# Two-layer PEER decoder step: turns of one gathered row instead of two, and weights formed at the end of a row's own turn

## What is computed

```python
# layer 0 mixer
z = gelu(x @ w_in); u, v = split(z); v = layer_norm(v)
y = (u * (tril(w_s) @ v + bias)) @ w_out
# layer 1 mixer
b, c, h = split(x @ w_in); z = c * h
y = (b * conv3(z)) @ w_out
# PEER, both layers, per token
q = (x @ w_query).reshape(8 heads, 2, 128)
s = q . sub_keys                       # 128 keys on each of 2 sides
sv, si = top_k(s, 16)                  # each side
cv, ci = top_k(all 16*16 sums, 16)     # 16 experts of 16384 per head
idx = i1 * 128 + i2;  g = softmax(cv)
a = gelu(expert_u[idx] . x)
out = sum over 8 heads, 16 experts of  g * a * expert_v[idx]
```

## Time and profile before

| what | value |
|---|---|
| runs | 1817.57, 1815.79, 1817.54 us; median 1817.54 |
| the profiled execution | 1816.76 us; span 1814.9 us |
| mean granted TensorE clock in it | 0.799 of full speed |
| TensorE, VectorE, ScalarE, GpSimd busy | 75%, 67%, 16%, 38% of the span |
| gathered by the indirect DMAs | 604.02 MB in 576 rows |
| moved in all | 718.27 MB |

### The profile page before, as it was taken

How to read it: one execution, slowest core, us unless ns; L and a number is a source line. 1 busy time by engine, 2 the same in 40 slices (tenths; PEclk the granted TensorE clock), 3 DMA queues, 4 the chain that set the end, 5 groups by cost and what they waited for, 6 DMA issues and landing times.

```text
span 1814.9 us, 23000 instructions
## 1 busy us (share of the span) xinstructions
PE 1358.0 (75%) x8388; PEld 644.8 (36%) x8388; DVE 1219.2 (67%) x3197; ACT 289.8 (16%) x970; POOL 684.7 (38%) x580
## 2 busy tenths in 40 slices
PE   8997989988946978776664498788765666776743
PEld 6884556644601744521110176356111111111100
DVE  1238867655648868678887656566888965555565
ACT  1111231102112202111111111021111100000011
POOL 0013423333223423344545533433444444444453
PEclk9998999999965989977665599989876667666655
DMA  9749999999999999999999999999999999999996
GB/s 381 293 154 422 381 362 393 356 422 420 409 423 417 380 421 421 420 410 422 408 422 393 421 340 418 422 418 420 407 421 411 397 421 421 421 421 421 417 420 282
DMA packets 100657, 718.27 MB, mean 396 GB/s; under 512 B 12064, under 2 KB 12576, under 8 KB 13600
## 3 DMA queue, kind: packets, MB, share of 16 engines
q0 software_dynamic: 82944, 604.02, 81.2%
q1 hardware_dynamic: 17184, 112.19, 15.2%
q10 hardware_dynamic: 416, 0.60, 0.1%
HBM read 715.24 MB, written 1.52 MB: 395 GB/s over the span
## 4 chain that ended last, share of the span: by engine, by line
DMA 48%; PE 34%; DVE 8%; issue 6%; DVEq 2%; POOL 2%; ACT 1%; another core or an unknown queue 0%; SPq 0%; POOLq 0%
DMA uvring<-expert_uv_dram,idx 43%; PE psum L649 11%; PE psum L660 11%; DMA wring<-w_chunks_dram 5%; PE psum L779 4%; PE psum L692 3%; DVE uvring L1190 2%; POOL uvring L601 2%; DVE diag L1203 1%; PE psum L731 1%; PE psum L762 1%; PE psum L759 1%; PE psum L668 1%; PE psum L641 1%; DVEq L993 1%
## 5 line engine op out<-in xcount | busy, mean ns | idle before, releaser
L601 POOL DMA_INDIRECT uvring<-expert_uv_dram,idx x576 | 684.5, 1188 | 1108.0 <-PE psum L649 872.9
L1190 DVE SCALAR_TENSOR_TENSOR uvring<-uvring,xn 128x1024 f32<-128x1024 f32 x576 | 705.5, 1225 | 413.0 <-DMA uvring<-expert_uv_dram,idx 394.1
L649 PE MATMUL psum<-uvring,diag 64*64 64x512 f32 x4096 | 709.6, 794 | 315.6 <-DVE diag L1203 305.7
L649 PEld LDWEIGHTS psum<-uvring,diag 64*64 64x64 f32 x4096 | 137.6, 159 | 805.2 <-DVE diag L1203 718.6
L908 ACT ACTIVATE a_gelu<-a_raw 128x1 f32<-128x1 f32 x576 | 114.8, 202 | 1205.7 <-DVE uvring L1190 1203.0
L660 PE MATMUL psum<-xT,wring 128*128 128x160 f32 (+1 forms) x1696 | 236.6, 298 | 27.5 <-DMA wring<-w_chunks_dram 26.5
L660 PEld LDWEIGHTS psum<-xT,wring 128*128 128x128 f32 x1696 | 223.2, 196 | 70.0 <-DMA wring<-w_chunks_dram 38.0
L1203 DVE TENSOR_SCALAR diag<-twin,a_gelu,gate 128x64 f32<-128x64 f32 x512 | 159.4, 311 | 26.8 <-ACT a_gelu L908 24.4
L641 PE MATMUL psum<-uvring,diag 128*32 128x256 f32 x512 | 68.9, 634 | 90.6 <-DVE diag L1203 85.7
L828 ACT ACTIVATE arena<-psum 128x160 f32<-128x160 f32 (+2 forms) x160 | 46.1, 298 | 225.6 <-PE psum L660 179.4
L779 PE MATMUL psum<-wring,arena 128*128 128x256 f32 x288 | 70.3, 400 | 3.4 <-DMA wring<-w_chunks_dram 2.3
(11 more groups left out here) (117 smaller groups left out, 836.1 us busy)
## 6 DMA issues: line engine op xcount, KB each, us to landing
wring<-w_chunks_dram SPq DMA_DIRECT2D x73, 1024.0 KB
uvring<-w_chunks_dram SPq DMA_DIRECT2D x15, 1024.0 KB, 9.8
kept<-w_chunks_dram SPq DMA_DIRECT2D x12, 1024.0 KB, 15.6
uvring<-expert_uv_dram,idx POOLq DMA_INDIRECT x576
x<-x_tok_dram SPq DMA_DIRECT2D x2, 512.0 KB, 4.6
uvring<-ln_gain_dram SPq DMA_DIRECT2D x1, 1024.0 KB, 28.5
uvring<-ln_bias_dram SPq DMA_DIRECT2D x1, 1024.0 KB, 28.9
keys<-sub_keys_dram SPq DMA_DIRECT2D x2, 512.0 KB, 9.7
```

The source lines that it names most:

```text
L601: pool.indirect_dma_start(uvring[:, n % RING, :], None, expert_uv, bass.IndirectOffsetOnAxis(ap=idx[t][:, i:i + 1], axis=0),).then_inc(uv_ ...
L649: mm = nc.tensor.matmul(acc[64 * j:64 * j + 64, 512 * i:512 * (i + 1)], diag[64 * i:64 * i + 64, place % DIAGS, :], row[64 * i:64 * i + 64 ...
L1190: nc.vector.scalar_tensor_tensor(out=uvring[:, slot, 0:D], in0=uvring[:, slot, 0:D], scalar=1.0, in1=xn[t][:, :], op0=ALU.mult, op1=ALU.mu ...
```

## The change

A turn becomes one row. `ROOM` is given per row, smaller than half of what a pair had, and a step that overdraws an engine's room is paid back from the next turns (`credit`); unused room isn't kept. VectorE takes at most one routing part in two turns, and one in each turn when the due turn is near. In turn p the engines now run:
- VectorE: dot p, steps, weights p.
- ScalarE: gelu p, steps.
- TensorE: row p (the first row of a tile waits for the next turn), steps.

So the weights of a row stand behind its own dot and behind the turn's steps, where they stood behind the next row's dot. A score read waits for part 1 of the routing that last read these scores (a new semaphore, `scanned`), and the planner knows of it. Code that could put a row's v half on VectorE (`VEC`, `add_v`, `wgt`), which no row used, is gone. The ring, the gathers, the chunks and the arithmetic are the same. The diff, cut to its core:

```diff
@@ -114,6 +104,15 @@
 
     heads = HEADS if t < 2 else FHEADS
     return ([(0, 1), (1, 1)] if (l, t) == (0, 0) else [(0, 2)]) + [(i, 2) for i in range(2, heads, 2)]
+
+
+def scanned_before(l, t, first, count):
+
+    before = [(l, 0) if t == 1 else (l - 1, 2 if t == 2 else 1)][0]
+    if before not in ITEM0:
+        return None
+    last = first // 2 + (count - 1) // 2 if t < 2 else 0
+    return *before, max(i for i, _ in calls_of(*before) if i <= last)
 
 
 def mixer_steps(n):
...
@@ -210,10 +209,12 @@
         for b0, count in scores_of(l, tiles[0]):
             if b0 + count - 1 == b:
                 out.append(("PE", ("s", l, tiles[0], b0, count), 0.9, [("q read", n, b)]))
-                out.append(("ACT", ("s read", l, tiles[0], b0, count), 0.6, [("s", l, tiles[0], b0, count)]))
+                scanned = scanned_before(l, tiles[0], b0, count)
+                out.append(("ACT", ("s read", l, tiles[0], b0, count), 0.6,
+                            [("s", l, tiles[0], b0, count)] + ([("route", *scanned, 1)] if scanned else [])))
     if 2 in tiles:
         out.append(("PE", ("s", l, 2, 0, HP), 2.0, [("q read", n, HP - 1)]))
-        out.append(("ACT", ("s read", l, 2, 0, HP), 0.6, [("s", l, 2, 0, HP)]))
+        out.append(("ACT", ("s read", l, 2, 0, HP), 0.6, [("s", l, 2, 0, HP)] + [("route", 0, 2, 0, 1)] * l))
     return out
 
...
 
+
 ROOM = {
-    (0, 0): {"DVE": 2.8, "ACT": 4.0, "PE": 5.0},
-    (0, 1): {"DVE": 2.4, "ACT": 3.0, "PE": 3.6},
-    (0, 2): {"DVE": 2.4, "ACT": 3.0, "PE": 3.6},
-    (1, 0): {"DVE": 2.6, "ACT": 3.0, "PE": 4.2},
-    (1, 1): {"DVE": 2.4, "ACT": 3.0, "PE": 3.6},
-    (1, 2): {"DVE": 2.4, "ACT": 3.0, "PE": 3.6},
+    (0, 0): {"DVE": 1.3, "ACT": 2.0, "PE": 1.85},
+    (0, 1): {"DVE": 1.2, "ACT": 1.5, "PE": 1.4},
+    (0, 2): {"DVE": 1.2, "ACT": 1.5, "PE": 1.4},
+    (1, 0): {"DVE": 1.2, "ACT": 1.5, "PE": 1.5},
+    (1, 1): {"DVE": 1.2, "ACT": 1.5, "PE": 1.5},
+    (1, 2): {"DVE": 1.2, "ACT": 1.5, "PE": 1.5},
 }
 
 
 def due(k):
 
-    return PAIR0[k[1], k[2]] + k[3] * TOPK // 2 - RING // 2 - 1
+    return ITEM0[k[1], k[2]] + k[3] * TOPK - RING - 2
 
 
 def plan_steps():
+
 
 
     early = [s for s in mixer_steps(1) if s[1][1:3] == ("mix", 0) or s[1][0].startswith("xT") and s[1][2] == "mix"]
@@ -281,8 +284,8 @@
     routing = [s for lti in order[1:] for s in route_steps(*lti)]
 
     turn = {("start",): -2}
-    for lt, p in END.items():
-        turn["vdone", *lt] = p + 1
+    for lt, n in LAST.items():
+        turn["vdone", *lt] = n + 1
     by = {k: e for e, k, _, _ in ahead + dense + routing}
     plan = {e: {-1: [k for who, k, _, _ in ahead if who == e]} for e in ENGINES}
     turn |= {k: -1 for _, k, _, _ in ahead}
...
@@ -299,39 +302,47 @@
         if e == "PE" and group_of(k) not in opened:
 
             was = opened[-BANKS]
-            return turn.get((READ[was[0]], *was[1:], *([2] if was[0] == "of" else [])), 2 * PAIRS) <= p
+            return turn.get((READ[was[0]], *was[1:], *([2] if was[0] == "of" else [])), 2 * len(ITEMS)) <= p
         return True
 
-    p = 0
+    p, credit, routed_at = 0, {e: 0.0 for e in ENGINES}, -2
     while any(q for e in ENGINES for q in queues[e]):
-        room = ROOM[ITEMS[2 * p][:2]] if p < PAIRS else {e: 1000.0 for e in ENGINES}
+        room = ROOM[ITEMS[p][:2]] if p < len(ITEMS) else {e: 1000.0 for e in ENGINES}
         for e in ENGINES:
-            spent, parts, plan[e][p] = 0.0, 0, []
+            credit[e] = min(credit[e], 0.0) + room[e]
+            plan[e][p] = []
             while True:
                 mine = [q for q in queues[e] if q and ready(e, q[0][1], q[0][3], p)]
+                hurry = False
                 if e == "DVE" and mine and mine[-1][0][1][0] == "route":
 
                     k = mine[-1][0][1]
-                    if due(k) - p < 9 - k[4] + 3:
+                    hurry = due(k) - p < 9 - k[4] + 8
+                    if hurry:
                         mine = mine[::-1]
-                    elif parts:
+                    elif p < routed_at + 2:
                         mine = mine[:-1]
-                if not mine or spent > 0 and spent + mine[0][0][2] > room[e] + 0.5:
+                if not mine or credit[e] <= 0.1 and not hurry:
                     break
                 _, k, cost, _ = mine[0].pop(0)
-                spent, parts = spent + cost, parts + (k[0] == "route")
+                credit[e] -= cost
+                if k[0] == "route":
+                    routed_at = p
                 turn[k] = p
                 plan[e][p].append(k)
+                if hurry and due(k) - p > 8 - k[4]:
+                    break
                 if e == "PE" and group_of(k) not in opened:
                     opened.append(group_of(k))
         p += 1
     for k, at in turn.items():
         assert k[0] != "route" or at < 0 or at <= due(k), (k, at, due(k))
+        assert k[0] != "recip" or at < 0 or at <= due(k) + RING, (k, at, due(k))
     return plan, turn, p
 
 
 PLAN, TURN, TURNS = plan_steps()
-TURNS = max(TURNS, PAIRS + 1)
+TURNS = max(TURNS, len(ITEMS) + 2)
 
...
@@ -812,8 +820,8 @@
 
             for p in range(-1, TURNS):
 
-                for n in (2 * p - 2, 2 * p - 1, 2 * p):
-                    if 0 <= n < 2 * PAIRS and not VEC[n] and (n in ITEM0.values()) == (n == 2 * p - 2):
+                for n in (p - 1, p):
+                    if 0 <= n < len(ITEMS) and (n in ITEM0.values()) == (n == p - 1):
                         weigh(n)
                 for k in PLAN["PE"].get(p, []):
                     do(k)
...
@@ -872,11 +880,9 @@
                     read(("q", n, b), qT[:, b, 0:WIDTH[n]], ACT.Copy, WIDTH[n])
                 elif kind == "s read":
                     _, l, t, first, count = k
-
-                    if t == 2 and l:
-                        act.wait_ge(routed, ROUTES.index((0, 2, 0)) + 1)
-                    if t < 2 and (l, t) != (0, 0):
-                        act.wait_ge(routed, ROUTES.index((l, 0, 6) if t else (l - 1, 1, 6)) + 1)
+                    before = scanned_before(l, t, first, count)
+                    if before:
+                        act.wait_ge(scanned, ROUTES.index(before) + 1)
                     key = ("s", l, t, first, count)
...
@@ -927,10 +933,9 @@
             for k in PLAN["ACT"][-1]:
                 do(k)
             for p in range(TURNS):
-                if p < PAIRS:
-                    gelu(2 * p)
-                    gelu(2 * p + 1)
-                for lt, end in END.items():
+                if p < len(ITEMS):
+                    gelu(p)
+                for lt, end in LAST.items():
                     if p == end + 1:
                         turn_sum(*lt)
                 for k in PLAN["ACT"].get(p, []):
...
+                    done = dve.drain()
+                    if signal:
+                        done.then_inc(signal, 1)
 
                 if part == 0:
                     dve.wait_ge(scalar_read, G[scores_for(l, t, i)][3])
                     first8(sides)
                 elif part == 1:
-                    next8(sides)
+
+                    next8(sides, scanned)
                 elif part == 2:
                     V.tensor_copy(tif[:, 0:2 * H, :], ti[:, 0:2 * H, :])
                     for m in range(H):
...
@@ -1196,32 +1204,15 @@
                 _, t, i = ITEMS[n]
                 c = n % (2 * TOPK)
                 dve.wait_ge(gelu_done, n + 1)
-                if not VEC[n]:
-                    place = RANK[n]
-                    if place >= DIAGS:
-                        dve.wait_ge(v_tensor, place - DIAGS + 1)
-                    nc.vector.tensor_scalar(diag[:, place % DIAGS, 0:32 if t == 2 else 64],
-                                            fold[:, :] if t == 2 else twin[:, :], a_gelu[:, c:c + 1],
-                                            gate[t][:, i:i + 1], ALU.mult, ALU.mult).then_inc(diag_ready, 1)
-                else:
-                    nc.vector.tensor_tensor(wgt[:, c:c + 1], a_gelu[:, c:c + 1], gate[t][:, i:i + 1], ALU.mult
-                                            ).then_inc(w_ready, 1)
-
-            def add_v(n):
-                _, t, _ = ITEMS[n]
-                c = n % (2 * TOPK)
-                dve.wait_ge(w_ready, RANK[n] + 1)
...
@@ -1247,25 +1238,21 @@
             after(did(nc.vector.tensor_tensor(twin[:, :], ident[:, 0:64], ident[:, 64:P], ALU.add)))
             for p in range(TURNS):
 
-                if p < PAIRS and 2 * p in ITEM0.values():
-                    l, t, _ = ITEMS[2 * p]
+                if p in ITEM0.values():
+                    l, t, _ = ITEMS[p]
                     wait_norm(dve, "ffn", l, t)
                     if t == 2:
                         dve.wait_ge(xn2_spread, (FOLD - 1) * (l + 1))
 
-                for n in (2 * p, 2 * p + 1):
-                    if n < 2 * PAIRS:
-                        dot(n)
-                    if 1 <= n <= 2 * PAIRS:
-                        weigh(n - 1)
-                for n in (2 * p - 1, 2 * p):
```

(27 more changed lines are left out.)

36 lines of the change are left out of this document (15 added, 21 removed).

## The result

| what | before | after |
|---|---|---|
| runs beside each other, median | 1817.55 us | 1848.71 us (four runs: 1840.37 to 1855.41) |
| ratio to before | 1 | 1.0164, 95% interval 1.0135 to 1.0192 |
| the profiled execution | 1816.76 us, span 1814.9 | 1843.39 us, span 1841.2 |
| mean granted TensorE clock | 0.799 | 0.812 |

The forecast was 13 us faster, with a range that ended at 1821. The changed kernel is 31 us slower by the medians, 26.3 by the two profiled spans, and the traces are read against the latter. Work did not grow much: on the page of the changed kernel (busy time by engine, then the DMA total, then the chain's shares) TensorE, VectorE and the bytes stand close to the earlier trace rows.

A forecast was written before the change was run, and what follows sets the result against it. DMA was taken as the bound: 421 GB/s ceiling, 1706 us for all bytes, the rest lost for lack of requests. 17 us gained less 2 + 0.2 + 2 gave 13 us, to 1804.5 us; range 1786 to 1821.

The forecast's parts named there:

- (a): Even plan: less TensorE room per row where dense steps use kept chunks; losses of 23.6 become 6.6, 17 us gained.
- ScalarE's reads follow their block by a turn, as before: ScalarE in the new order: its reads keep their one-turn distance from TensorE's block; no cost charged.
- (b): New order on VectorE: steps waiting for TensorE stand ahead of weights; charged for mixing, layer-norm rows and gelu, nothing for adds.
- Mixing: Eight spatial mixing rows: 4.0 us each, 32 us, 38 with routing parts; loss taken as 9 instead of 7.0.
- layer-norm rows: Eight layer-norm events of two tiles: nothing to 8 us lost, taken as 4 instead of 3.8.
- rival 4: TensorE's clock falls in even turns: about 1865 us; chance 0.03.
- the prediction's own mark, over 36 us: Sign in the eight mixing rows: over 36 us shows rival 3's mechanism, even if the total does not.
- rival 3: Slower: VectorE's step waiting for TensorE, with routing behind it, stands ahead of the weights; +9, 1827 us; chance 0.12.
- Adds: 20 residual adds, 1.4 us each: nothing lost, as DMA takes 1.5 to 2 us more than TensorE there.
- Gelu: Weights waiting 0.34 us for the row's own gelu where no step stands in the turn: 2 us taken.
- point of decision: Rival 3 decides where idle passes a stretch's DMA excess over TensorE work, some 8 us for layer-norm rows.

The follow-up runs named there:

- e13: The kernel before, its two-row turns and order kept, with only the even plan added (smaller room per pair, overdrafts paid back): 1798.48 us, ratio 0.9874.
- e9: e7 with the old plan's room per row (TensorE 2.5, 1.8, 2.1; VectorE 1.4, 1.2, 1.3): 1826.46 us, ratio 1.0031.
- e7: The changed kernel, weights last, with VectorE and ScalarE using a TensorE step only two turns later: 1802.74 us, ratio 0.9912.
- e3: The changed kernel, weights last, with VectorE steps using a TensorE step only two turns later: 1807.3 us, ratio 0.9935.
- e5: The changed kernel with VectorE reading TensorE two turns late and weights right behind the own dot: 1834.67 us, ratio 1.0094.
- e4: The kernel before with only the weights of row 2p moved behind the turn's steps: 1860.62 us, ratio 1.0216.
- e8: The changed kernel with three more overwritten bias products per mixing step of the second pass: 1870.0 us, ratio 1.0296.
- e11: e7 with weights of rows whose turn has no VectorE step put behind the next row's dot: 1800.14 us, ratio 0.9883.
- e1: The changed kernel with a row's weights right behind its own dot, ahead of the turn's steps: 1837.6 us, ratio 1.0105.

## Why the prediction was wrong

**(a) held.** 17 us were forecast, e13 shows 23 alone and e9 against e7 22. In the changed kernel about half of it, 9 us, is visible: rows 288 to 320 went from 9.0 to 3.2 (forecast 9.1 to 2.1 for that stretch) and 128 to 144 from 3.1 to none, but rows 16 to 48 stayed at 13.8. There, ScalarE's reads of the turn before hold the gelus; e7 brings 8.7. The step "ScalarE's reads follow their block by a turn, as before" overlooked that a turn is now half as long.

**(b), the order on VectorE, is the step that failed**, in two of its terms.
- Mixing. The row at full clock was right: 4.0 us forecast, 3.94 measured, with 0.80 us of idle for the forecast's 0.99. The eight rows were put at 32 to 38 us and took 43, because from 380 on they ran at half clock; the loss was put at 9, and rows 48 to 80, which hold mixing and layer-norm rows, lost 32.6 instead of 9 + 4. I had priced a falling clock as rival 4, for even dense turns, where it did not happen (rows 80 to 128 ran at 1.00), and had not put it in the mixing rows. It could have been seen there: the prediction says that the clock is 0.92 to 1.00 where TensorE is over 90% busy, but its own row of 320 to 360 has 40.00 us busy of 40 at 0.91. Behind that mean the clock was at half from about 337 to 343, and the 29.7 us of before hold that stretch too. By the prediction's own mark, over 36 us, rival 3's mechanism is there.
- Adds were "nothing", since DMA needs 1.5 to 2 us more than TensorE there. Rows 160 to 176 lost 14.4. That cover assumes that requests stay out while TensorE idles; with the wait ahead of the weights the slots come back late, and the routing part in the next turn adds 3.77 us to 1.21. e3 loses none here, so the late wait is what the term left out; how much of the 14.4 is the lower clock in these rows (0.76 against e3's 0.88) stays open. Behind the adds of tile (0,0) four turns (rows 77, 82, 88 and 94) took 9.1 to 10.8 us from dot to dot; there the forecast's cover held for the most part, for rows 80 to 128 lost nothing.
- Gelu, 2 us: right for the changed kernel (rows 176 to 288 lost less than before, 2.8 against 5.8), since the turn's steps cover it. Without that cover it is 27 us (e5 against e3); "0.34 fits, barely" was no margin.

**Rival 3** had the mechanism and the sign but not the size (+9 against +31), nor its chance of 0.12. Its point of decision, idle passing what DMA has to spare, compares totals of a stretch. e3 shows that what decides is slack in turns: one turn more between TensorE's step and VectorE's read, and the same work in the same order loses nothing in rows 64 to 80 and 160 to 176. e4 shows what one turn was worth before: with both weights of a pair ahead of the steps, TensorE had up to two rows to do while VectorE waited.

The Trainium skill, TensorE: Matmul & The Clock Gate, section "HAM oscillation", says that idle between groups of matmuls drops the clock. The traces agree in part: in e7, e8 and the changed kernel idle of 0.80 to 1.82 us at a time came before the fall, and in e3, where TensorE hardly paused, the clock held. They go against it in the kernel before, where it fell after some 15 us without a pause. I used the rule on the plan's evenness, and in the even turns of rows 80 to 128 nothing of the kind was seen.

**Left open.** The four runs of the changed kernel lie at 1840, 1843, 1854 and 1855, those of e7 at 1797 twice and 1808 twice. For e7, whose profile is of an execution at 1808, mixing at full and at half clock would fit the two groups. For the changed kernel it would not, for its profile, with mixing at half clock, is of one of the faster two. In both kernels the mean granted clock of a slower execution is lower than that of a faster one (0.803 and 0.806 against 0.812 and 0.814; 0.813 twice against 0.817 and 0.815), but in which rows it was lower is not known. What lifts the clock again was not tried. That e11 and e13 could be joined, with pairs and late reads, was not tried either.

## What to carry to other kernels

Where an in-order engine waits for another one and also makes what that other needs next, the order of the two decides whether they overlap: put the product first, if its own inputs are there by then (e1 and e5 paid for that), or schedule the wait two turns later (e3). A plan's "one turn later" is time, so halving the turn halves every slack in it; count the loop around the two engines, not each engine's busy share. Even out dense work against a steady transfer stream on its own; here e13 gains 1.3% by that alone, and the changed order lost more than that.

## What the hardware showed that I had not expected

The granted clock stayed at 0.50 for some 30 us in e7 while TensorE was busy 10.00 us of every 10, and in e8 at 18.39 of 20; the same mixing in e3 ran at 1.00. A loop that leaves only 0.80 us idle in 3.94 us was followed by the fall, and in the kernel before the fall came without any idle in the 15 us ahead of it. So a stretch in which TensorE is busy all the time, by the busy share, can still take nearly twice as long (5.62 us per row in e7 against 3.06 in e3). A mean of 0.91 over 40 us hid such a fall; it shows in short windows.
